# An encoder layer on one core: tokens turned by VectorE instead of TensorE in the projection, with three smaller edits merged in

## The chip, the cores and the metric

The kernel runs on one core of a Trainium2 chip. The metric is the device time of one execution in microseconds (us). A core has five engines that work side by side, each in its own written order: TensorE (PE, matrix products and 128x128 transposes), VectorE (DVE), ScalarE (ACT), GpSimd (POOL) and SyncE (SP, which only issues DMAs here). They wait for each other through semaphores.

## The reference, cut to what matters

One encoder layer over 3,072 tokens (2,048 and 1,024) of 1,024 numbers, in float32. The change touches the normalisation ahead of the first product, rope and, in small ways, what comes after.

```python
def rmsnorm(x, g):
    y = x * lax.rsqrt(jnp.mean(x * x, axis=-1, keepdims=True) + EPS)
    return y * g

def encoder(x, mem, ...):
    z = rmsnorm(x, g_mix) @ w_in                     # 1024 -> 2304 columns
    q_a, k_a = rope(z[..., :512]), rope(z[..., 512:1024]); v_a = z[..., 1024:1536]
    o_a = dilated_attention(q_a, k_a, v_a)           # three patterns, 8 heads
    u, v = split(gelu(z[..., 1536:2048]))            # gMLP: layernorm(v), mixed over 128 tokens
    o_b = u * (w_spatial @ layernorm(v) + b_spatial)
    o_c = softmax(z[..., 2048:] @ k_mem.T) @ v_mem   # attention to 256 memory rows, 4 heads
    x = x + concat(rmsnorm(o_a), rmsnorm(o_b), rmsnorm(o_c)) @ w_out
    x = x + expert_choice(rmsnorm(x, g_ffn), ...)    # 16 experts, each takes its top tokens
    return rmsnorm(x, g_final)
```

## The kernel before, in words

The phases follow each other with a barrier between them: memory (keys and values of the memory rows, and `w_in` split into two parts), projection, attention, mix (`w_out`, norms, router), choice of tokens, experts. Every product in full precision is three passes over a high and a low part of both operands (`hi`, `lo`).

**Projection** (`project_phase`, L321) loops over 24 tiles of 128 tokens, two to a pass of the loop. Each engine has its order written out by hand. TensorE's for tile t: z_qc, the turn of tile t-1's k into [column, token] (`turn_k`, L663), `back` (L669), z_uv, the turn of qc (L695), z_q, the scores to memory (L702), **the turn of tile t+1's x** (`turn`, L656, eight 128x128 transposes into the PSUM tile `ps_x`), z_k, the turn of q (L711), the spatial product (L718, waits for `vln`), the turn of the probabilities (L726, waits for `p_sb`), z_v and the product with the memory's values. All z are `product`, L676.

Before x of tile t+1 is turned, ScalarE squares it (L451) with a sum over its columns, VectorE makes the mean (`mean_x`, L553), GpSimd the power -1/2 (`prep`, L425) and ScalarE scales x by it (`scale_x`, L455). In the [token, column] layout one token is one partition, so a sum is one number per partition. After the turn ScalarE copies `ps_x` out as the high part (`hi_x`, L460) and VectorE subtracts for the low part (`lo_x`, L557).

Beside that runs the chain of gelu and layernorm: ScalarE squares uv (`uv_sq`, L494), VectorE makes `inner` (L587, L589), ScalarE takes the exp (L503), VectorE one plus it, its reciprocal (L593), the product `guv`, mean and variance (L598 to L604), and, behind the rotation of q (`rotate`, L567 and L571) and the row maximum of the scores (L610), `vln` (L618, L622). On ScalarE the scaling of x stands ahead of that exp, and `hi_x` behind it. The exponentials of the scores (L511) give `p_sb`.

SyncE stores v, obc, and the turned q and k of a tile, one DMA each with runs of 512 bytes (L397 to L404), and loads x two tiles ahead (L126).

**Memory phase** (`memory_phase`, L130): SyncE loads `w_in` in 24 pieces of 128 rows and 768 columns (L190), ScalarE and VectorE split each into its two parts (L210, L252). **Mix** (L1113): 24 tiles again; its first loads are issued at its own start (L1171, L1200). **Experts** (L1852): 16 experts of 12 units each; SyncE loads the weights in quarters (L1563). The final norm of 24 token tiles is worked into the last two experts: tile t is loaded at the unit `FIN_AT[t]` (L1957) and squared on ScalarE one unit later (L2110). The first of them in the last expert waits for the previous expert's scatter:

```python
if t == 0 or FIN_AT[t - 1] < M <= FIN_AT[t]:
    sp.wait_ge(s["scattered"], 16 * ST * e)
```

Of the kernel before, what the change touches and what calls it, by code (L numbers as in the profile page):

```python
# [114 lines left out]
class Tokens:  # L115


    def __init__(self, keep):
# [4 lines left out]
        self.s = {n: keep.sem(n) for n in "squared_x meaned_x powered_x scaled_x".split()}  # L123

    def load(self, sp, A, t, u):
        sp.dma_start(self.x[:, u, :], A["x"][bass.ds(t * P, P), :]).then_inc(self.x_loaded[u], 16)  # L126
        sp.dma_start(self.cs[:, u, :, :], A["cossin"][bass.ds(t * P, P), :]).then_inc(self.x_loaded[u], 16)


def memory_phase(nc, A, kmT, vm, w_hi, w_lo, tok):  # L130
# [9 lines left out]
    with Phase(nc, "mem") as ph:  # L140
# [4 lines left out]
        junk = ph.sb("junk", [P, D], BF16)  # L145
# [4 lines left out]
        stat = ph.sb("stat", [P, 3])  # L150
# [7 lines left out]
        ssx, msx, rsx = stat[:, 0:1], stat[:, 1:2], stat[:, 2:3]  # L158
# [12 lines left out]
        with nc.Block() as block:  # L171
            @block.sync
            def _(sp):
# [10 lines left out]
                rows(2)  # L184
                for q in range(PIECES):
# [11 lines left out]
            def _(pool):  # L197
# [5 lines left out]
                nc.gpsimd.tensor_tensor(rsx, msx, half[:, 0:1], ALU.pow).then_inc(tok.s["powered_x"], 1)  # L203

            @block.scalar
            def _(act):
                def hi(q):
                    k, cols = piece(q)
                    act.wait_ge(in_loaded[q % RI], 16 * (q // RI + 1))
# [8 lines left out]
                def square(n):  # L218
                    act.wait_ge(m_loaded[n], 16)
                    ge(act, squared, n)  # L220
                    nc.scalar.activation(junk[:], m[:, n % 2, :], ACT.Square, accum_out=ss[:, n:n + 1]).then_inc(squared, 1)
# [11 lines left out]
                act.wait_ge(tok.x_loaded[0], 32)  # L233
                act.wait_ge(squared, NM)
                nc.scalar.activation(junk[:], x[:, 0, :], ACT.Square, accum_out=ssx).then_inc(tok.s["squared_x"], 1)
# [3 lines left out]
                nc.scalar.activation(x[:, 0, :], x[:, 0, :], ACT.Copy, scale=rsx).then_inc(tok.s["scaled_x"], 1)  # L239
# [3 lines left out]
            def _(dve):  # L243
# [32 lines left out]
                dve.wait_ge(tok.s["squared_x"], 1)  # L276
                nc.vector.tensor_scalar(msx, ssx, 1.0 / D, EPS, ALU.mult, ALU.add).then_inc(tok.s["meaned_x"], 1)
# [6 lines left out]
            def _(pe):  # L284
# [27 lines left out]
                for n in range(NM):  # L312
# [3 lines left out]
                    if n:  # L316
                        turn_k(n - 1)
                turn_k(NM - 1)


def project_phase(nc, A, kmT, vm, w_hi, w_lo, tok):  # L321

    with Phase(nc, "prj") as ph:
# [4 lines left out]
        PADS = 2 * len(SEQS) * PAD // P  # L328
        qkv = ph.sb("qkv", [P, 3, D_A])
# [6 lines left out]
        oc = ph.sb("oc", [P, D_C])  # L336
# [9 lines left out]
        half = ph.sb("half", [P, 2])  # L346
# [475 lines left out]
def attention_blocks():  # L822
# [9 lines left out]
    return blocks  # L832


def attend_phase(nc, A, w_out):

# [1574 lines left out]
```

## Time and profile before

| | |
|---|---|
| median of 3 runs | 3372.18 us (3369.89 to 3373.27) |
| the profiled execution | 3375.52 us, of which the span of the trace is 3373.7 |
| granted TensorE clock, mean of the span | 0.973 |
| busy share of the span | PE 95%, DVE 50%, ACT 43%, POOL 21% |
| projection, from its first to its last instruction | about 53 to 811 us |
| attention, mix, choice of tokens, experts | from about 815, 1,271, 1,645 and 1,708 us |

Busy shares are means over phases with different limits. A granted clock of 1.00 is 2.4 GHz, 0.50 is 1.2 GHz.

### The profile page before, as it was taken

The page shows a single profiled execution, that of the slowest core. Times are in us where ns is not written, and L with a number is a line of the kernel's source. Part 1 is how long each engine was busy: PE and PEld are TensorE (multiplying, and loading weights), DVE is VectorE, ACT ScalarE, POOL GpSimd, SP SyncE. Part 2 cuts the span into 40 slices and gives each one's busy share as a digit, 9 for nine tenths or more (in the row PEclk, how much of TensorE's full clock was granted, in tenths as well). Part 3 has the DMA queues.
Part 4 walks back from the last instruction along what each step waited for, and adds up shares of the span by engine and source line. Part 5 has one row for each costly group of instructions (what it writes and reads, how often), then busy time and mean ns, then how long its engine had stood idle before and what let it go on. Part 6 is the DMA issues. An engine that isn't in the chain of part 4 may idle for free. (4 is left out here: it accounts for less than half of the span.)

```text
span 3373.7 us, 57007 instructions
## 1 busy us (share of the span) xinstructions
PE 3209.9 (95%) x21676; PEld 2892.8 (86%) x21676; DVE 1675.1 (50%) x3594; ACT 1450.6 (43%) x3106; POOL 696.6 (21%) x726
## 2 busy tenths in 40 slices
PE   7999999997999996999579999999999999999996
PEld 5888888886777775888479999999999999999996
DVE  5445445543677775555554443444443444443454
ACT  4333333333788883333333333333333333333443
POOL 0111111112312112222122112222112222112422
PEclk9999999998999997999779999999999999999998
DMA  5111111114744444555347666677666677667895
GB/s 208 59 49 55 51 58 50 48 59 127 248 120 116 127 106 148 191 194 187 113 134 157 137 159 164 164 164 159 137 157 164 164 164 161 136 156 164 231 271 192
DMA packets 345874, 476.41 MB, mean 141 GB/s; under 512 B 31296, under 2 KB 258368, under 8 KB 345536
## 3 DMA queue, kind: packets, MB, share of 16 engines
q1 hardware_dynamic: 324928, 404.34, 43.7%
q0 software_dynamic: 20736, 69.22, 8.3%
q8 instruction: 138, 2.26, 0.3%
q14 instruction: 72, 0.59, 0.1%
HBM read 361.44 MB, written 112.00 MB: 140 GB/s over the span
## 5 line engine op out<-in xcount | busy, mean ns | idle before, releaser
L2127 DVE TENSOR_TENSOR warm_lo<-warm_stage,warm_hi 128x2048 fp32r<-128x2048 f32 x192 | 440.1, 2293 | 596.3 <-ACT warm_hi L1568 596.2
L1568 ACT ACTIVATE warm_hi<-warm_stage 128x2048 fp32r<-128x2048 f32 x192 | 366.5, 1909 | 0.0
L2266 PE MATMUL exp_ps_g<-exp_xT_hi,warm_lo 128*128 128x384 f32 x1024 | 343.1, 335 | 9.7 <-DVE warm_lo L2127 8.2
L2266 PE MATMUL exp_ps_g<-exp_xT_lo,warm_hi 128*128 128x384 f32 x1024 | 342.7, 335 | 0.0
L2266 PE MATMUL exp_ps_g<-exp_xT_hi,warm_hi 128*128 128x384 f32 x1024 | 342.6, 335 | 0.0
L2266 PE MATMUL exp_ps_u<-exp_xT_hi,warm_lo 128*128 128x384 f32 x1024 | 342.0, 334 | 0.0
L2266 PE MATMUL exp_ps_u<-exp_xT_hi,warm_hi 128*128 128x384 f32 x1024 | 342.0, 334 | 0.0
L2266 PE MATMUL exp_ps_u<-exp_xT_lo,warm_hi 128*128 128x384 f32 x1024 | 342.0, 334 | 0.0
L2001 POOL DMA_INDIRECT scratch_y<-exp_ye,route_slots x45 | 92.3, 2052 | 1009.6 <-issue 924.1
L1040 ACT ACTIVATE att_prob<-att_prob,att_o 128x256 f32<-128x256 f32 (+1 forms) x576 | 265.8, 465 | 71.8 <-DVE att_o L1084 68.6
L1976 POOL DMA_INDIRECT exp_xe<-scratch_xn,exp_rows_of x180 | 225.0, 1250 | 55.1 <-issue 54.5
L2083 ACT ACTIVATE exp_hT_hi<-exp_hid 128x768 fp32r<-128x768 f32 x64 | 54.2, 846 | 416.9 <-DVE exp_hid L2160 416.9
L2283 PE MATMUL exp_ps_d<-warm_hi,exp_hT_hi 128*128 128x256 f32 x768 | 217.3, 283 | 0.0
L2283 PE MATMUL exp_ps_d<-warm_hi,exp_hT_lo 128*128 128x256 f32 x768 | 217.3, 283 | 0.0
L2283 PE MATMUL exp_ps_d<-warm_lo,exp_hT_hi 128*128 128x256 f32 x768 | 217.2, 283 | 0.0
L1084 DVE CUSTOM_DVE_ANT_0 att_prob<-att_ps_s,att_masks 128x256 f32<-128x256 f32 (+1 forms) x576 | 183.6, 375 | 40.2 <-issue 40.1
L2266 PEld LDWEIGHTS exp_ps_g<-exp_xT_hi,warm_lo 128*128 128x128 f32 x1024 | 192.8, 188 | 10.2 <-DVE warm_lo L2127 8.5
L2266 PEld LDWEIGHTS exp_ps_g<-exp_xT_lo,warm_hi 128*128 128x128 f32 x1024 | 192.9, 188 | 0.0
L2266 PEld LDWEIGHTS exp_ps_g<-exp_xT_hi,warm_hi 128*128 128x128 f32 x1024 | 192.7, 188 | 0.0
L2266 PEld LDWEIGHTS exp_ps_u<-exp_xT_hi,warm_lo 128*128 128x128 f32 x1024 | 192.2, 188 | 0.0
L2266 PEld LDWEIGHTS exp_ps_u<-exp_xT_lo,warm_hi 128*128 128x128 f32 x1024 | 192.2, 188 | 0.0
L2266 PEld LDWEIGHTS exp_ps_u<-exp_xT_hi,warm_hi 128*128 128x128 f32 x1024 | 192.2, 188 | 0.0
(341 smaller groups left out, 7739.4 us busy)
## 6 DMA issues: line engine op xcount, KB each, us to landing
warm_stage<-in_w_gate SPq DMA_DIRECT2D x256, 256.0 KB, 5.1
warm_stage<-in_w_up SPq DMA_DIRECT2D x256, 256.0 KB, 5.3
warm_stage<-in_w_down SPq DMA_DIRECT2D x256, 256.0 KB, 3.9
mix_o<-scratch_o SPq DMA_DIRECT2D x72, 264.0 KB, 3.0
att_v<-scratch_v SPq DMA_DIRECT2D x64, 256.0 KB, 3.9
scratch_xn<-mix_xn SPq DMA_DIRECT2D x24, 544.0 KB, 3.0
memory_x<-in_x SPq DMA_DIRECT2D x24, 512.0 KB, 3.3
att_v<-scratch_v SPq DMA_DIRECT2D x192, 64.0 KB, 2.2
```

Of the source, the lines that this page charges most:

```text
L1040: x_ = nc.scalar.activation(p, p, ACT.Exp, bias=o[:, c % RO, h:h + 1], scale=-1.0, accum_out=o[:, c % RO, HA + h:HA + h + 1])
L1084: x_ = nc.vector.tensor_tensor_reduce(out=prob[:, n % RP, jj, f, 0:b.W], in0=ps_s[:, n % 2, f, jj, 0:b.W], in1=masks[:, b.mask, 0:b.W], sc ...
L1568: self.nc.scalar.activation(self.hi[:, m % self.RW, :, :], self.stage[:, m % self.RS, :, :], ACT.Copy).then_inc(self.hi_sb, 1)
L1976: nc.gpsimd.indirect_dma_start(xe[:, e % 2, j, a * Q_COLS:(a + 1) * Q_COLS], None, quarters, bass.IndirectOffsetOnAxis(ap=rows_of[:, a, at ...
L2001: nc.gpsimd.indirect_dma_start(A["y"], bass.IndirectOffsetOnAxis(ap=slots[:, j, e:e + 1], axis=0), ye[:, j, :], None, compute_op=ALU.add). ...
L2083: nc.scalar.activation(hT_hi[:, 2 * j:2 * j + 2, :], hid[:], ACT.Copy).then_inc(s["h_hi_sb"], 1)
L2127: nc.vector.tensor_tensor(w_lo[:, m % RW, :, :], stage[:, m % RS, :, :], w_hi[:, m % RW, :, :].bitcast(F32), ALU.subtract).then_inc(s["w_l ...
L2266: x_ = nc.tensor.matmul(ps[:, f, 0:S], a[:, m % RW, k, f * P:(f + 1) * P], b[:, k, :], start=(n == 0), stop=(n == 3 * KC - 1))
L2283: x_ = nc.tensor.matmul(down_banks[j][q][:, 0:UC], b[:, k, rows], a[:, m % RW, k, :], start=(k == 0 and n == 0), stop=(k == KC - 1 and n = ...
```

## The change: what it does, and the diff

The projection loads x of a tile in four DMAs, one for each quarter of the columns. Quarter b lies on partitions 32b to 32b+31, and a token's four quarters lie on four partitions (a token is a lane r of 32 and a group a). In this layout one transposition of every 32x32 block, which VectorE does in one instruction, gives the [column, token] layout that the products want. The rows of `w_in` are loaded in the matching order, by four DMAs a piece, and `g_mix` is laid out to match. The sum of squares of a token now lies on four partitions; a product on TensorE with the constant `lanes` adds them. So squaring, mean, power and scaling each handle four numbers per partition or four quarters. Mean and scaling keep their place in the order of ScalarE; the mean moves behind `inner` on VectorE, `turn_x` stands behind the variance. q and k are likewise turned in 32x32 blocks by VectorE and put right by their stores, four DMAs each with runs of 128 bytes. The factor of the scores goes into the rotation of q, which uses scalar_tensor_tensor. The buffer of oc becomes a part of obc. TensorE's transposes of x, q and k and ScalarE's copies of turned q and k fall away.

Merged with it: the first loads of the mix are issued inside attention, into space that the queries of the first sequence no longer need (`Early`), and the mix's first weighting goes ahead of its weight split; the first expert turns the first half of the columns of all tokens first (`FIRST`), and its first unit waits for half of them at a time; the final-norm tiles of the last expert are loaded later (`FIN_AT`).

```diff
 class Tokens:
     def load(self, sp, A, t, u):
-        sp.dma_start(self.x[:, u, :], A["x"][bass.ds(t * P, P), :]).then_inc(self.x_loaded[u], 16)
+        for b in range(QUADS):
+            sp.dma_start(self.x[b * QR:(b + 1) * QR, u, :].rearrange("t (a c) -> t a c", c=QD),
+                         A["x"][bass.ds(t * P, P), b * QD:(b + 1) * QD].rearrange("(a t) c -> t a c", t=QR)).then_inc(self.x_loaded[u], 16)
@@ memory_phase, SyncE @@
                 for q in range(PIECES):
-                    sp.dma_start(stage[:, q % RI, :], A["w_in"][k * P:(k + 1) * P, cols]).then_inc(in_loaded[q % RI], 16)
+                    for b in range(QUADS):
+                        rows_b = A["w_in"][b * QD + k * QR:b * QD + (k + 1) * QR, cols]
+                        sp.dma_start(stage[b * QR:(b + 1) * QR, q % RI, :], rows_b).then_inc(in_loaded[q % RI], 16)
                     if q == 2 * PER - 1:
+                        sp.wait_ge(squared, NM)
                         tok.load(sp, A, 0, 0)
@@ project_phase, SyncE @@
+                def store_turned(name, which, t, stored):
+                    for a in range(BLOCKS):
+                        part = A[name][:, :, bass.ds(t * P + a * B32, B32)].rearrange("(c i) j t -> i j c t", i=B32)
+                        sp.dma_start(part, qkv[a * B32:(a + 1) * B32, which, :].rearrange("i (j c t) -> i j c t", c=BLOCKS, t=B32))\
+                            .then_inc(stored, 16)
                         sp.wait_ge(s["rotk_sb"], t + 1)
-                            sp.wait_ge(s["xT"], t + 1)
+                            sp.wait_ge(s["lo_sb"], t + 1)
                             tok.load(sp, A, t + 2, u)
+                        sp.wait_ge(s["q_turned"], t + 1)
+                        store_turned("qT", 0, t, q_stored)
@@ project_phase, GpSimd @@
+                        if not is_first(t):
+                            root_bc(t - 1)
                         if not (last and u):
                             prep(t + 1)
-                        if not is_first(t):
-                            root_bc(t - 1)
@@ project_phase, ScalarE @@
                 def square_x(t, u, n):
-                    nc.scalar.activation(probT[:], x[:, u, :].rearrange("p (k c) -> p k c", c=P), ACT.Square, accum_out=ssx).then_inc(s["squared_x"], 1)
+                    for a, x_a in enumerate(tok.quarters(u)):
+                        x_ = nc.scalar.activation(probT[:, 2 * a:2 * a + 2, :], x_a.rearrange("p (k c) -> p k c", c=P), ACT.Square,
+                                                  accum_out=ssx[:, a:a + 1])
+                    x_.then_inc(s["squared_x"], 1)
                 def scale_x(t, u):
                     act.wait_ge(s["powered_x"], t + 1)
-                    nc.scalar.activation(x[:, u, :], x[:, u, :], ACT.Copy, scale=rsx).then_inc(s["scaled_x"], 1)
+                    for a, x_a in enumerate(tok.quarters(u)):
+                        x_ = nc.scalar.activation(x_a, x_a, ACT.Copy, scale=rsx[:, a:a + 1])
+                    x_.then_inc(s["scaled_x"], 1)
                 def hi_x(t, u):
-                    act.wait_ge(s["xT"], t + 1)
+                    act.wait_ge(s["x_turned"], t + 1)
...
-                        if not is_first(t):
-                            out_k(t - 1)
...
-                        nc.scalar.activation(qkv[:, 0, :], ps_c[:], ACT.Copy, scale=SCALE).then_inc(s["qT_sb"], 1)
@@ project_phase, VectorE: functions @@
+                def turn_x(t, u):
+                    dve.wait_ge(s["scaled_x"], t + 1)
+                    nc.vector.transpose(x[:, u, :], x[:, u, :]).then_inc(s["x_turned"], 1)
                 def mean_x(t):
-                    nc.vector.tensor_scalar(msx, ssx, 1.0 / D, EPS, ALU.mult, ALU.add).then_inc(s["meaned_x"], 1)
+                    nc.vector.tensor_scalar(msx, ps_x[:, 0, 0:QUADS], 1.0 / D, EPS, ALU.mult, ALU.add).then_inc(s["meaned_x"], 1)
+                def turn32(which, t, added, done):
+                    dve.wait_ge(added, t + 1)
+                    nc.vector.transpose(qkv[:, which, :], qkv[:, which, :]).then_inc(done, 1)
...
-                        last_a = nc.vector.tensor_tensor(ah[:, :, j, :], zh[:, :, j, :], cos, ALU.mult)
+                        last_a = nc.vector.scalar_tensor_tensor(out=ah[:, :, j, :], in0=zh[:, :, j, :], scalar=scale, in1=cos, op0=ALU.mult, op1=ALU.mult)
@@ project_phase, VectorE: order of a tile @@
-                        if more:
-                            mean_x(t + 1)
                         if not is_first(t):
                             mean_bc(t - 1)
+                            turn32(1, t - 1, s["rotk_sb"], s["k_turned"])
...
                         nc.vector.tensor_tensor(uv_b[:], uv_b[:], ps_b[:], ALU.mult).then_inc(s["inner"], 1)
+                        if more:
+                            mean_x(t + 1)
...
                         nc.vector.tensor_scalar(vev, mv[:, 1:2], EPS, None, ALU.add).then_inc(s["var_eps"], 1)
+                        if more:
+                            turn_x(t + 1, 1 - u)
                         dve.wait_ge(s["z_q"], t + 1)
...
                         if more:
                             lo_x(t + 1, 1 - u)
-                        ge(dve, k_stored, 16 * t)
+                        ge(dve, k_stored, 16 * BLOCKS * t)
+                        turn32(0, t, s["rotq_sb"], s["q_turned"])
@@ project_phase, TensorE @@
+                def sum_x(t):
+                    pe.wait_ge(s["squared_x"], t + 1)
+                    nc.tensor.matmul(ps_x[:, 0, 0:QUADS], tok.lanes[:], ssx, start=True, stop=True).then_inc(s["summed_x"], 1)
...
-                        if not is_first(t):
-                            turn_k(t - 1)
                         product(ps_b, u, 3 * D_A, 2 * D_B).then_inc(s["z_uv"], 1)
+                        if not (last and u):
+                            sum_x(t + 1)
...
-                        if not (last and u):
-                            turn(t + 1, 1 - u)
                         product(ps_a, u, D_A, D_A).then_inc(s["z_k"], 1)
-                        pe.wait_ge(s["rotq_sb"], t + 1)
-                        for j in range(HA // 2):
-                            x_ = nc.tensor.transpose(ps_c[:, j * P:(j + 1) * P], qkv[:, 0, j * P:(j + 1) * P], ident[:])
-                        x_.then_inc(s["qT_ps"], 1)
                         pe.wait_ge(s["vln_sb"], t + 1)
@@ attend_phase, SyncE (LEFT: blocks of the first sequence, RO: buffers of the outputs) @@
+                    if c == LEFT + RO - 1:
+                        sp.wait_ge(q_set, LEFT - 1)
+                        for t in range(2):
+                            early.load_o(sp, A, t, t)
+                        early.load_x(sp, A, 0, 0)
+                        sp.dma_start(early.g_out, A["g_out"]).then_inc(early.g_loaded, 16)
+                        sp.dma_start(early.ident, A["ident"]).then_inc(early.id_loaded, 16)
@@ mix_phase, ScalarE @@
+                weigh(0)
                 act.wait_ge(g_loaded, 16)
-                hi_w(0)
-                weigh(0)
-                hi_w(1, 2, 3, 4, 5)
+                hi_w(0, 1, 2, 3, 4, 5)
@@ expert_phase @@
-        FIN_AT += [M + m for m in (1, 1, 2, 3, 3, 4, 5, 5, 6)]
+        FIN_AT += [M + m for m in (3, 3, 4, 4, 5, 5, 6, 6, 6)]
+        FIRST = [r for half in range(2) for r in range(half, ROUNDS, 2)]
...
-                            if m == 0:
+                            if m == 0 and e:
                                 pe.wait_ge(s["xT_lo_sb"], ROUNDS * (e + 1))
+                                        if e == 0 and m == 0 and f == 0 and k % 4 == 0:
+                                            pe.wait_ge(s["xT_lo_sb"], ROUNDS // 2 * (k // 4 + 1))
```

## Rows read from the trace of the kernel before

**Rows 1.** Stretches: us; busy of PE, PEld, DVE, ACT, POOL; PEclk, DMA share, GB/s.

```profile
200.00:231.15 31.15, 31.15 (x181) 26.04 (x181) 14.81 (x32) 11.19 (x27) 4.34 (x5) 1.00 0.16 53
```

**Rows 2.** Timeline of PE, one projection tile: start us, us, engine, line, out<-in, shape.

```profile
230.03 1.10 PE L656 MATMUL prj_ps_x<-memory_ident,memory_x 128*128 128x128 f32 x8
230.88 0.48 PE L676 MATMUL prj_ps_a<-memory_w_hi,prj_hT_lo 128*128 128x512 f32 x1
...
236.44 0.60 PE L711 MATMUL prj_ps_c<-memory_ident,prj_qkv 128*128 128x128 f32 x4
236.88 1.00 PE L718 MATMUL prj_ps_o<-prj_vln,prj_wsT 128*128 128x64 f32 x8
237.72 1.04 PE L726 MATMUL prj_ps_x<-memory_ident,prj_prob 128*128 128x128 f32 x8
```

**Rows 3.** Timeline of ACT, the same tile.

```profile
220.81 0.51 ACT L475 ACTIVATE prj_obc<-prj_uv_b,prj_stat 128x256 f32<-128x256 f32 x1 [1.12 <-POOL prj_stat L420]
221.22 0.49 ACT L476 ACTIVATE prj_obc<-prj_oc,prj_stat 128x256 f32<-128x256 f32 x1
...
225.18 0.63 ACT L503 ACTIVATE prj_uv_a<-prj_uv_b 128x512 f32<-128x512 f32 x1
...
235.85 0.21 ACT L511 ACTIVATION_READ_ACCUMULATOR prj_prob<-prj_ps_s,prj_stat 128x1 f32 x1
```

**Rows 4.** Timeline of DVE, the same tile.

```profile
224.46 0.69 DVE L589 TENSOR_TENSOR prj_uv_b<-prj_uv_b,prj_ps_b 128x512 f32<-128x512 f32 x1
...
231.10 0.15 DVE L604 TENSOR_SCALAR prj_stat<-prj_stat 128x1 f32<-128x1 f32 x1
231.28 0.76 DVE L567 TENSOR_TENSOR prj_qkv<-prj_ps_c,memory_cs 128x256 f32<-128x256 f32 x2
...
234.52 0.48 DVE L622 SCALAR_TENSOR_TENSOR prj_vln<-prj_vln,prj_stat,prj_ln_b 128x256 f32<-128x256 f32 x1
```

**Rows 5.** Timeline of POOL, memory phase.

```profile
21.66 1.04 POOL L201 TENSOR_TENSOR mem_rstd<-mem_ms,mem_half 128x4 f32<-128x4 f32 x1 [20.82 <-DVE mem_ms L271]
```

**Rows 6.** Groups by line, DVE: busy us, mean ns of one, idle before.

```profile
L2135 DVE STREAM_TRANSPOSE exp_act_g<-exp_xe 128x512 f32<-128x512 f32 x45 | 31.7, 704 | 0.0
```

**Rows 7.** DMA issues at the mix's start: KB each, median us to landing.

```profile
mix_w_r<-in_w_router SPq DMA_DIRECT2D x1, 64.0 KB, 7.2
```

**Rows 8.** Timeline of SP's DMA issues, memory phase and one weight tile.

```profile
6.99 2.62 SPq L190 DMA_DIRECT2D mem_stage<-in_w_in  x5
...
28.13 16.98 SPq L190 DMA_DIRECT2D mem_stage<-in_w_in  x12
...
1718.91 1.91 SPq L1563 DMA_DIRECT2D warm_stage<-in_w_gate  x4
```

**Rows 9.** Timelines of SP and DVE, start of the mix.

```profile
1270.71 1.32 SPq L1171 DMA_DIRECT2D mix_o<-scratch_o  x3
...
1276.61 0.18 DVE L1354 TENSOR_REDUCE mix_stat<-mix_o 128x8 f32<-128x24 f32 x1 [10.34 <-DMA mix_obc<-scratch_obc]
```

**Rows 10.** Timeline of PE, first product of the first expert.

```profile
1725.57 0.41 PE L2266 MATMUL exp_ps_g<-exp_xT_hi,warm_lo 128*128 128x384 f32 x1 [1.56 <-DVE exp_xT_lo L2146]
```

**Rows 11.** Timelines of SP, ACT and PE, last expert.

```profile
3268.15 0.82 SPq L1957 DMA_DIRECT2D exp_fin<-scratch_y  x2
...
3291.65 1.06 ACT L2110 ACTIVATE exp_fin_junk<-exp_fin 128x1024 bf16<-128x1024 f32 x1 [10.72 <-DMA exp_fin<-scratch_y]
...
3300.58 0.69 PE L2266 MATMUL exp_ps_g<-exp_xT_hi,warm_lo 128*128 128x384 f32 x1 [8.15 <-DVE warm_lo L2127]
```

**Rows 12.** PE in the mix, and slices (as rows 1) around two gaps.

```profile
1306.36 0.90 PE L1461 MATMUL mix_ps_c<-mix_ident,mix_oa 128*128 128x128 f32 x3 [5.64 <-ACT mix_oa L1277]
...
1303.00:1304.00 1.00, 0.00 (x0) 0.00 (x0) 0.00 (x0) 0.00 (x0) 0.98 (x1) 0.86 0.00 0
...
3297.00:3298.00 1.00, 0.00 (x0) 0.00 (x0) 0.00 (x0) 1.00 (x1) 0.57 (x1) 0.55 1.08 388
...
3303.00:3304.00 1.00, 1.00 (x5) 1.00 (x5) 1.00 (x2) 0.00 (x0) 1.00 (x2) 0.53 1.03 385
```

More of the change, by code:

```diff
@@ L157, in memory_phase @@
         psK = ph.psum("psK", [P, 4, P])
-        ssx, msx, rsx = stat[:, 0:1], stat[:, 1:2], stat[:, 2:3]
+        ssx, msx, rsx = (stat[:, n * QUADS:(n + 1) * QUADS] for n in range(3))
+        lanes_loaded = ph.sem("lanes_loaded")
         m_loaded = [ph.sem(f"m_loaded{n}") for n in range(NM)]
@@ L317, in _ @@
                         turn_k(n - 1)
+                    if n == NM - 2:
+                        pe.wait_ge(lanes_loaded, 16)
+                        pe.wait_ge(turned_sb, NM - 1)
+                        pe.wait_ge(tok.s["squared_x"], 1)
+                        nc.tensor.matmul(psT[:, 0, 0, 0:QUADS], tok.lanes[:], ssx, start=True, stop=True).then_inc(tok.s["summed_x"], 1)
                 turn_k(NM - 1)
@@ L335, in project_phase @@
         ob = uv_b[:, 0:D_B]
[L336 removed]
+        oc = obc[:, D_B:]
         qc = ph.sb("qc", [P, D_C])
@@ L847, in attend_phase @@
     NU = 2 * NB
+    LEFT = sum(b.seq == 0 for b in blocks)
     with Phase(nc, "att") as ph:
@@ L1169, in load_o @@
                     ge(sp, s["cT_ps"], t - 1)
-                    for j in range(3):
-                        sp.dma_start(o3[:, u, j, :], A[f"o{j}"][bass.ds(t * P, P), :]).then_inc(o_loaded[u], 16)
-                    sp.dma_start(obc[:, u, :], A["obc"][bass.ds(t * P, P), :]).then_inc(o_loaded[u], 16)
+                    early.load_o(sp, A, t, u)
                 def load_x(t, u, n):
@@ L2210, in _ @@
                                         table.pick[:, at:at + 1], ALU.mult, ALU.add).then_inc(s["rows_set"], 1)
-                for r in range(ROUNDS):
-                    lo_x(r, first_banks[r % len(first_banks)])
+                for n, r in enumerate(FIRST):
+                    lo_x(n, r, first_banks[n % len(first_banks)])
                 for m in range(1, RW - 1):
@@ L2286, in _ @@
                 spread_rows()
-                for r in range(ROUNDS):
-                    turn(r)
+                for n, r in enumerate(FIRST):
+                    turn(n, r)
                 pe.wait_ge(s["rows_set"], 1)
@@ L2317, in build @@
             if upto >= 2:
-                attend_phase(nc, A, w_out)
+                early = Early(nc, out)
+                attend_phase(nc, A, w_out, early)
             if upto >= 3:
-                mix_phase(nc, A, affinity, w_out)
+                mix_phase(nc, A, affinity, w_out, early)
         with Phase(nc, "warm") as warm:
```

185 lines of the change are left out of this document (99 added, 86 removed).

## The prediction

> **What bounds the kernel now.** I read the table of stretches first, for one steady token tile of the projection. It shows TensorE busy for the whole 31.15 us period at a granted clock of 1.00, VectorE and ScalarE at less than half of it [rows 1]. So an instruction taken off TensorE there is worth its pitch, and a wait put on it costs its length. The timeline of TensorE in the next tile [rows 2] gives the pitches and the place of the first two waits: the spatial product (L718) waits for `vln`, the transposes of the probabilities (L726) for `p_sb`. The timelines of ScalarE and VectorE [rows 3, 4] show the chain that makes both: gelu's exp (L503), reciprocal, variance (L604), rotation of q (L567), row maximum, `vln` (L622 ends 235.00) and the last exponential's sum (ends 236.06). TensorE gets to the place of L711 at 236.44. With L711 gone, that is where L718 would start. The slack on `vln` is thus 236.44 - 235.00 = 1.44 us.
>
> **Projection: TensorE's own work.** Removed per tile: eight transposes of x (230.03 to 230.88, 0.85 us), four of q (236.44 to 236.88, 0.44) and four of k, which I take at the 0.43 of q's [rows 2]: 1.72 us. Added: one product with `lanes`, four columns wide. The nearest row is L718, where eight records of 64 columns take 236.88 to 237.72, 0.105 us each; two records, as a pair of that row's four groups has, make 0.21. Net -1.51 us a tile, if nothing waits.
>
> **Projection: the chain to `vln`.** Three edits lengthen it. VectorE and ScalarE work in their written order, so nothing of the chain can pass them.
> First, the scaling of x. `mean_x` now stands behind `inner` on VectorE and reads PSUM; `inner` ends at 224.46 + 0.69 = 225.15 [rows 4]. The mean takes the 0.15 of L604, GpSimd's power of 128x4 takes 1.04 [rows 5], and I allow 0.05 for each of three hand-overs (L503 starts 0.03 behind `inner`): 226.49. Then come four scalings of 256 columns on ScalarE, whose pitch is that from L475 to L476, 0.41 [rows 3]: 226.49 + 1.64 = 228.13. Only then does ScalarE reach gelu's exp, which before began at 225.18: 2.95 us later. In the old order mean and power lay ahead of the square of uv, in the wait for z_uv, and the scaling alone stood before the exp.
> Second, `turn_x` stands between the variance and the rotation of q. The nearest row is a 32x32-block transpose of half the width, 0.704 us [rows 6]. Twice that is 1.41, once is the bound below; I take 1.3, as the work grows with columns and a small part doesn't.
> Third, the rotation's four products become scalar_tensor_tensor: 0.48 (L622, as wide) against 0.38 (half of L567's 0.76) [rows 4]; between 0 and 0.4 in all, and 0.2 taken because L622 reads SBUF alone.
> Together 2.95 + 1.3 + 0.2 = 4.45 us (3.65 to 4.76). TensorE meanwhile arrives 0.85 - 0.21 = 0.64 earlier, so 0.80 of slack is left and it stalls 4.45 - 0.80 = 3.65 us (2.85 to 3.96) ahead of L718. Late next is `p_sb`: it comes at 236.06 + 4.45 = 240.51, while L718, released at 239.45, ends 0.84 later at 240.29: another 0.2. A tile costs -1.51 + 3.65 + 0.2 = +2.34 us (1.35 to 2.65). The next chain starts from the next z_uv, so nothing of it is won back. For the 23 tiles that prepare a successor: 53.8; the last saves 0.9 on q and k: **+53 us** (30 to 60).
> Costed at nothing: the quarter squares, the turn of k and the turn of q in 32x32 blocks on VectorE, and `lo_x` from SBUF. The squares and the turn of k lie in the stretch in which ScalarE and VectorE wait for z_uv (L476 ends at 221.71, `inner` starts at 224.46). The turn of q comes behind `vln`, and between L726 and the product that needs VectorE's last copy TensorE has another whole product, z_v (5.56 us, as z_k from 230.88 to 236.44). Without that cover each turn costs 0.7 us a tile. That oc and obc now share a buffer makes VectorE's write of oc wait for the last store of obc, issued a tile before.
>
> **Projection: SyncE.** The eight stores of q and k of a tile now move runs of 128 bytes, 512 to a store. The nearest row for such pieces is a load of 1,024 runs of 64 bytes, landed in 7.2 us with other loads around it [rows 7]: at half of it for each of four, 14.4 us. The stores of k are issued ahead of `inner` (224.46) and asked for behind `vln` (now 239.45), at `turn32(0)`: 15 us. So I cost them at nothing, with little to spare. The load of x goes out later in the tile by the chain's delay; that too I cost at nothing, and a late x would hold ScalarE ahead of `uv_sq` as a late store holds VectorE. The Trainium skill ("DMA: Bandwidth & Descriptors", Specifications) says that transfers under 512 bytes don't reach line rate; by that this edit turns stores that cost nothing into a possible bound, and the time would be that of the rival below. That row is the only one that bears on it, and it leaves room.
>
> **Memory phase.** SyncE issues at 0.52 us a piece (2.62 for five) up to 0.48 (1.91 for a weight tile's four), starts w_in at 6.99 and ends at 45.11 [rows 8]. Before, buffers paced it; now 96 quarter loads, `lanes`, the last memory rows and five loads of x make 103 issues, at 0.478: 49.2, so 56.2 instead of 45.1. **+11 us** (+7 at the 0.44 of the mix's loads [rows 9], +16 at 0.52). Behind the last load stands the split of that piece as before.
>
> **Ends of phases.** k of the last tile goes out in four stores, not one: 3 x 0.48, **+1.4**. The first join of the mix waits for its loads, issued from 1270.71, until 1276.61 [rows 9]; with `Early` they lie in SBUF: **-5.9** (weigh(0) first may add under 1 us; a late landing takes it all). The first expert waits 1.56 us for the last `lo_x` [rows 10], which the new order of rounds can save: **-1.5** (0 to -1.6). In the last expert ScalarE stands until 3291.65 on a final-norm tile, loaded behind SyncE's issue at 3268.15, which waits for a scatter with the weight loads queued behind it, and TensorE starves for 8.15 us up to 3300.58 [rows 11]; after it the clock is low until about 3303.95 [rows 12], 3.4 us at half speed, 1.7 lost. Two slots later the scatter is done when SyncE asks: **-9.8** (0 if the three loads crowded into the last slot block as long).
>
> **Sum.** 53 + 11 + 1.4 - 5.9 - 1.5 - 9.8 = +48 us, on the profiled execution's 3375.5: 3423.7. That execution is 3.3 us above the median of the runs shown, 3372.18, so in their terms **3420 us**; its own range is 3393 to 3442.
>
> **Rivals.**
> (a) *The clock falls in each stall.* At 1306.36 TensorE had been idle for 5.64 us, since 1300.72; the clock fell in the slice 1303 to 1304 (0.86), about 3.0 us into it. In the gap before 3300.58 it fell at about 3297.1 (0.55 in that slice), 4.7 us in [rows 11, 12]. A stall of 3.65 lies between the two. If it falls, 3.4 us of work go at 1.2 GHz, 1.7 us a tile: +39, 3459. The Trainium skill ("TensorE: Matmul & The Clock Gate", HAM oscillation) tells of a wait in every pass of a loop that brings the clock down in every pass: then this is the case. Against it: in the longer gap the clock held for 4.7 us, past the end of such a stall.
> (b) *TensorE stays the bound.* If the chain's three delays stay under the 0.80 of slack, each tile gives its 1.51 us: -36 + 11 + 1.4 - 17.2 = -41, 3331. It takes a ScalarE that gets to gelu's exp before the scaling, or delays a fifth of mine. The whole change breaks even at a stall of 1.7 us, `p_sb` included.
> (c) *Half the stall*, 1 to 2.3 us, by a `turn_x` near 0.7 and a scaling faster than its rows: 3358 to 3390.
> (d) *Small stores bind.* If pieces cost twice the bound of [rows 7], four stores of k need 28.8 us and come 13.8 late at `turn32(0)`. At most all of that reaches TensorE, and less by what z_v covers: some 10 x 23 = +230, 3650. For it speaks the size of the pieces alone; against it that nothing else is then on the queues.
>
> **Chances.** The forecast 0.53; (a) 0.18; (b) 0.14; (c) 0.11; (d) 0.04. About 0.2%, 7 us, is what a measurement of this kernel can tell from none; (c) is split over the three signs: faster 0.18, same 0.05, slower 0.77. The range runs from (c) to (a), 3362 to 3465, and leaves out (b) and (d).
>
> **What would show it.** In the changed profile: gelu's exp some 3 us behind the end of `inner`, not at once; TensorE idle about 3.6 us ahead of the spatial product, released by VectorE's `vln`; a projection tile of 33.5 us; granted clock near 1.00 through tiles (else (a)); SyncE's w_in issues end near 56; the mix's first reduction on VectorE within 1 us of its phase's start, not 5.9; no gap of TensorE in the last expert. The prediction fails if `vln` comes before TensorE asks for it, if the period stands at 29.7, or if SyncE's loads or stores release VectorE.

## The result, and the profile after

| | before | after |
|---|---|---|
| median | 3371.03 us (3368.90 to 3373.27, 4 runs) | 3457.01 us (3450.57 to 3461.04, 4 runs) |
| span of the profiled execution | 3373.7 us | 3459.3 us |
| granted TensorE clock, mean of the span | 0.973 | 0.959 |

The change makes the kernel 2.5% slower: ratio 1.0253, 95% interval [1.0235, 1.0271]. The forecast of 3420 had the direction; the time lies 15 us above the top of its own range, inside the whole one, and close to the 3459 of rival (a).

The waits of TensorE come first: engine, line, out, releaser, us in total, times, the longest. Before, `vln` was not among them.

```profile
PE prj_ps_o L757 <- DVE prj_vln L673: 67.2, 23, 3.0
PE mix_ps_c L1520 <- ACT mix_oa L1337: 21.8, 2, 16.7
...
PE mem_psT L341 <- ACT mem_rows L251: 12.7, 1, 12.7
...
PE exp_ps_g L2294 <- DVE exp_act_g L2266: 7.7, 1, 7.7
...
PE exp_ps_g L2329 <- DVE warm_lo L2188: 4.6, 1, 4.6
```

One steady projection tile as a stretch, with the columns of [rows 1]: 34.42 us in place of 31.15, TensorE idle for 3 us of it, and the clock at 0.95.

```profile
225.70:260.12 34.42, 31.46 (x167) 26.11 (x167) 16.83 (x35) 11.35 (x34) 4.81 (x5) 0.95 0.19 48
```

The chain inside such a tile, from the timelines of VectorE, GpSimd, ScalarE and TensorE (they answer to [rows 2 to 4]).

```profile
221.04 0.69 DVE L636 TENSOR_TENSOR prj_uv_b<-prj_uv_b,prj_ps_b 128x512 f32<-128x512 f32 x1
221.65 0.15 DVE L597 TENSOR_SCALAR prj_stat<-prj_ps_x 128x4 f32<-128x4 f32 x1
...
221.96 1.01 POOL L467 TENSOR_TENSOR prj_stat<-prj_stat,prj_half 128x4 f32<-128x4 f32 x1 [4.19 <-DVE prj_stat L597]
...
223.01 1.71 ACT L501 ACTIVATE memory_x<-memory_x,prj_stat 128x256 f32<-128x256 f32 x4 [2.18 <-POOL prj_stat L467]
224.62 0.62 ACT L544 ACTIVATE prj_uv_a<-prj_uv_b 128x512 f32<-128x512 f32 x1
...
230.59 1.23 DVE L592 STREAM_TRANSPOSE memory_x<-memory_x 128x1024 f32<-128x1024 f32 x1
231.75 0.72 DVE L615 SCALAR_TENSOR_TENSOR prj_qkv<-prj_ps_c,memory_cs 128x256 f32<-128x256 f32 x2
...
233.05 1.21 DVE L661 TENSOR_REDUCE prj_stat<-prj_ps_s 128x4 f32<-128x1024 f32 x1
...
234.92 0.48 DVE L673 SCALAR_TENSOR_TENSOR prj_vln<-prj_vln,prj_stat,prj_ln_b 128x256 f32<-128x256 f32 x1
...
235.46 1.67 PE L757 MATMUL prj_ps_o<-prj_vln,prj_wsT 128*128 128x64 f32 x8 [2.96 <-DVE prj_vln L673]
236.92 1.91 PE L765 MATMUL prj_ps_x<-memory_ident,prj_prob 128*128 128x128 f32 x8
```

`inner` ends at 221.73 and exp starts at 224.62: mean, power and four scalings stand between. (ScalarE squares and scales x in the places where it did before; the mean is VectorE's, and it is the mean that has moved.) `turn_x` puts 1.16 us ahead of the rotation (230.59 to 231.75). `vln` ends at 235.40, and TensorE has waited 2.96 us for it. L757 and L765 then take 1.46 and 1.91 us, where the same eight took 0.84 and 1.04 [rows 2]. The stretches around that wait say why; the last three columns are the granted clock, the DMA share and GB/s.

```profile
230.00:232.50 2.50, 2.50 (x12) 1.72 (x10) 2.42 (x8) 0.64 (x1) 0.55 (x1) 1.00 0.00 0
232.50:235.46 2.96, 0.00 (x1) 0.00 (x1) 2.89 (x7) 1.35 (x6) 1.26 (x1) 1.00 0.00 0
235.46:238.90 3.44, 3.44 (x17) 3.44 (x18) 3.44 (x9) 1.00 (x6) 0.36 (x1) 0.55 0.00 0
238.90:242.00 3.10, 3.10 (x14) 2.49 (x14) 1.01 (x4) 0.99 (x3) 0.92 (x1) 0.95 0.21 65
```

In the wait itself the clock stands at 2.4 GHz (1.00). It falls just after TensorE has begun again, and 3.44 us of work go at 0.55, nearly 1.2 GHz. That costs 0.45 x 3.44 + 0.05 x 3.10 = 1.70 us. A tile: 29.64 without waits (measured in experiment 5) + 2.96 + 1.70 + 0.12 not assigned = 34.42. Twenty tiles take 34.2 to 34.6 us. Three take 36: in them the clock stays low for 6.8 us, not 3.4. Over the 23 tiles the fall comes between 0.1 us before TensorE begins again and 1.7 us behind it.

The memory phase, by the timelines of SyncE and TensorE: the loads of `w_in`, at 0.46 to 0.47 us each (first and third row; the second holds waits for buffers), and the first projection product.

```profile
7.39 9.28 SPq L203 DMA_DIRECT2D mem_stage<-in_w_in  x20
...
20.14 16.01 SPq L203 DMA_DIRECT2D mem_stage<-in_w_in  x28
...
38.55 22.74 SPq L203 DMA_DIRECT2D mem_stage<-in_w_in  x48
...
72.13 0.58 PE L720 MATMUL prj_ps_a<-memory_w_hi,prj_hT_lo 128*128 128x256 f32 x1 [5.02 <-DVE prj_hT_lo L601]
```

The same product in the kernel before:

```profile
57.25 0.58 PE L676 MATMUL prj_ps_a<-memory_w_hi,prj_hT_lo 128*128 128x256 f32 x1 [2.37 <-DVE prj_hT_lo L557]
```

The last load of `w_in` is issued by 61.29, where 56.2 was predicted. Two stretches of the phase, with the columns as above:

```profile
20.00:30.00 10.00, 10.00 (x31) 4.94 (x30) 4.36 (x6) 4.47 (x6) 0.71 (x1) 1.00 1.05 218
...
40.00:50.00 10.00, 2.60 (x8) 1.03 (x6) 5.80 (x7) 3.92 (x5) 0.00 (x0) 0.73 0.73 207
```

The starts of the mix and of the first expert, and the last expert, which answer to [rows 9 to 11].

```profile
1368.96 0.18 DVE L1413 TENSOR_REDUCE mix_stat<-out_qT 128x8 f32<-128x24 f32 x1 [4.50 <-PEq L102]
...
1380.41 1.09 PE L1520 MATMUL mix_ps_c<-out_qT,mix_oa 128*128 128x128 f32 x4 [16.68 <-ACT mix_oa L1337]
...
1813.71 0.41 PE L2329 MATMUL exp_ps_g<-exp_xT_hi,warm_lo 128*128 128x384 f32 x1
...
3377.51 1.06 ACT L2178 ACTIVATE exp_fin_junk<-exp_xe 128x1024 bf16<-128x1024 f32 x1 [11.65 <-DMA exp_xe<-scratch_y,route_slots]
...
3385.20 0.69 PE L2329 MATMUL exp_ps_g<-exp_xT_hi,warm_lo 128*128 128x384 f32 x1 [4.63 <-DVE warm_lo L2188]
```

The mix's first reduction no longer waits for a DMA, the first expert starts without its 1.56 us, and in the last expert ScalarE stands as long as before, now for the gather of the fix tile (rows of the previous expert's tokens, which GpSimd gathers again for their final norm). TensorE's wait for the joined rows at the mix's start, now 16.7 us, was 23.3 before:

```profile
PE mix_ps_c L1461 <- ACT mix_oa L1277: 29.0, 2, 23.3
```

By marks on TensorE's timeline the 85.6 us of span are: first projection product +14.9, projection to `back` +79.1, gap to attention +1.2, attention +2.9, gap to the mix -6.65 (23.33 to 16.68), from there to the first expert -3.4, experts -2.6.

### The profile page after: what moved, and what is told of

The parts are those of the page before. It is cut to its first block and busy times, and to the rows that moved or that the text cites. A ratio compares the mean times of both kernels' runs of the same rounds, so it can differ in the third digit from the quotient of the medians.

```text
span 3459.3 us, 57179 instructions
## 1 busy us (share of the span) xinstructions
PE 3226.3 (93%) x21340; PEld 2896.6 (84%) x21340; DVE 1723.7 (50%) x3666; ACT 1454.5 (42%) x3274; POOL 703.7 (20%) x726
## 2 busy tenths in 40 slices
DMA packets 433571, 476.50 MB, mean 138 GB/s; under 512 B 134224, under 2 KB 349136, under 8 KB 433232
## 5 line engine op out<-in xcount | busy, mean ns | idle before, releaser
L2188 DVE TENSOR_TENSOR warm_lo<-warm_stage,warm_hi 128x2048 fp32r<-128x2048 f32 x192 | 440.1, 2293 | 599.6 <-ACT warm_hi L1627 599.6
```

Of the source, the lines that this page charges most:

```text
L2188: nc.vector.tensor_tensor(w_lo[:, m % RW, :, :], stage[:, m % RS, :, :], w_hi[:, m % RW, :, :].bitcast(F32), ALU.subtract).then_inc(s["w_l ...
```

## Experiments

Each ratio is to the kernel before on the same chip, with its 95% interval.

**1. The wait filled (e1).** Twelve passes of `w_hi` go into a free PSUM tile (PSUM is the memory that TensorE writes) between z_k and the wait for `vln`; their result is used nowhere.

```diff
                         product(ps_a, u, D_A, D_A).then_inc(s["z_k"], 1)
+                        if not (last and u):
+                            pe.wait_ge(s["guv"], t + 1)
+                            for n in range(12):
+                                nc.tensor.matmul(ps_b[:, 0:512], hT_hi[:, u, n % KC, :], w_hi[:, n % KC, 0:512], start=True, stop=True)
```

> The changed kernel with twelve useless passes of 512 columns (into the buffer of z_uv, once gelu is done with it) between z_k and the wait for vln; they take about 2.75 us of the 2.92 us in which TensorE stands there. What is computed stays the same. Theory A (each stall brings the clock down, and the slow stretch behind it costs 1.65 us a tile and 1.5 more in three tiles): a tile of 32.7 us, not 34.4, no slice at 1.2 GHz in the projection, about 42 us less than the changed kernel, 3415. Rival B (the slow stretch has another cause, such as the stores in small pieces or the share of short products): the tile stays at 34.4, 3457. Rival C (useless passes only push later work): the tile grows, 3460 or more.

Measured: 3416.27 us (3413.83 to 3418.38), 1.0117 [1.0100, 1.0134]. The wait that is left:

```profile
PE prj_ps_o L761 <- DVE prj_vln L673: 5.3, 23, 0.4
```

One tile, as a stretch:

```profile
227.07:259.96 32.89, 32.70 (x178) 26.86 (x178) 16.81 (x35) 11.36 (x37) 4.84 (x5) 1.00 0.19 50
```

TensorE comes to the spatial product as late as before (twelve passes of 0.227 us and 0.23 of wait on average make 2.95), and only the clock differs: 1.00, and 1.53 us less a tile. So of the 79 us some 40 are the clock's, and idleness brings it down.

**2 to 4. The chain shortened (e2, e3, e4).** e2 puts the mean ahead of `inner0`, so that the power runs beside VectorE's `inner`. e3 puts `turn_x` behind `vln`, `hi_x` behind the exponentials and `lo_x` to the end of the tile. e4 does both.

```diff
@@ e2, VectorE @@
+                        if more:
+                            mean_x(t + 1)
                         dve.wait_ge(s["uv_sq"], t + 1)
...
                         nc.vector.tensor_tensor(uv_b[:], uv_b[:], ps_b[:], ALU.mult).then_inc(s["inner"], 1)
-                        if more:
-                            mean_x(t + 1)
@@ e3, VectorE @@
                         nc.vector.tensor_scalar(vev, mv[:, 1:2], EPS, None, ALU.add).then_inc(s["var_eps"], 1)
-                        if more:
-                            turn_x(t + 1, 1 - u)
...
                         if more:
-                            lo_x(t + 1, 1 - u)
+                            turn_x(t + 1, 1 - u)
                         dve.wait_ge(s["z_k"], t + 1)
```

> The mean of the next tile's squares moved ahead of the first step of gelu's inner term on VectorE, so that power and scaling start 1.6 us earlier. Theory A: gelu's exp comes 1.6 us earlier, the stall ahead of the spatial product falls from 2.9 to about 1.3 us, which is too short for the clock to fall; a tile of about 31.2 us, 79 us less: 3378. Rival B (slow stretch not from the stall): a tile of 32.8, 37 us less: 3420. Rival D (the chain is not what TensorE waits for): no change, 3457.

> The turn of x on VectorE moved behind vln, the copy of its high part behind the exponentials of the scores, its low part to the end of the tile. Theory A: vln comes 1.2 us earlier, stall 1.7 us; if that holds the clock, a tile of 31.6 us, 69 us less: 3388. If the clock still falls, 33.2 us and 3430, which is also what rival B (slow stretch not from the stall) expects. Rival D: 3457.

> Both moves together. Theory A: 1.6 and 1.2 us off the chain leave a stall of about 0.2 us; TensorE sets the period, a tile of about 30.0 us against 31.15 before the change: about 106 us less than the changed kernel, 3351, faster than the kernel before the change. Rival B: 63 us less, 3394. Rival E (with the chain short, the stores or loads of x set the period): above 31 us a tile, with TensorE released through SyncE.

| version | wait for `vln` in a tile | tiles with a fallen clock | tile without / with the fall | us | ratio |
|---|---|---|---|---|---|
| after | 2.9 to 3.0 | 23 of 23 | - / 34.4 (three 36.0) | 3457.01 | 1.0253 [1.0235, 1.0271] |
| e3 | 1.8 to 2.0 | 14 of 23 | 31.9 / 33.5 | 3418.12 | 1.0126 [1.0110, 1.0143] |
| e2 | 1.3 to 1.5 | 8 of 23 | 31.4 / 33.0 | 3394.16 | 1.0049 [1.0033, 1.0066] |
| e4 | 0.26 to 0.50 | none | 30.4 / - | 3358.35 | 0.9942 [0.9926, 0.9959] |

The waits for `vln` in e2, e3 and e4, in that order:

```profile
PE prj_ps_o L757 <- DVE prj_vln L673: 32.4, 23, 1.5
...
PE prj_ps_o L757 <- DVE prj_vln L671: 43.9, 23, 2.0
...
PE prj_ps_o L757 <- DVE prj_vln L671: 9.2, 23, 0.5
```

The waits add up: e2 takes 1.5 us off, e3 1.0, both 2.5, so the two moves account for the wait but for a remnant. e2 and e3 came 16 and 30 us above what was expected of them, since I held waits of 1.4 and 1.9 us too short for the clock. They are not. The counts are those of the profiled execution; that of e3 took 3407.91 us, 10 less than its median, so the number of falls need not be the same in each. Two tiles of e2, each from the start of L757, the first behind a wait of 1.50 us and the second behind one of 1.33; a third, which starts at 413.37 behind a wait of 1.50, keeps its clock like the second:

```profile
284.60:286.00 1.40, 1.37 (x11) 1.28 (x12) 1.40 (x2) 1.04 (x6) 0.00 (x0) 1.00 0.00 0
286.00:288.10 2.10, 2.10 (x11) 1.91 (x9) 2.10 (x8) 0.00 (x0) 0.39 (x1) 0.53 0.00 0
...
317.50:319.00 1.50, 1.46 (x12) 1.37 (x13) 1.50 (x2) 1.05 (x6) 0.00 (x0) 1.00 0.00 0
319.00:321.00 2.00, 2.00 (x14) 1.74 (x13) 2.00 (x8) 0.00 (x0) 0.37 (x1) 1.00 0.00 0
```

**5. The sum halfway (e11).** On e4, with the fix tile of experiment 7: TensorE issues `sum_x` in the middle of z_uv, and ScalarE scales x ahead of the squares of uv.

```diff
                     for k in range(KC):
+                        if k == KC // 2 and halfway is not None:
+                            sum_x(halfway)
@@ ScalarE @@
+                        if more:
+                            scale_x(t + 1, 1 - u)
                         act.wait_ge(s["z_uv"], t + 1)
...
-                        if more:
-                            scale_x(t + 1, 1 - u)
```

> The version with the mean ahead of inner0 and the turn of x behind vln (3358 us), with the fix tile two slots later, and with the product over lanes halfway through z_uv and the scaling of x ahead of uv's squares on ScalarE. Theory A: the scaling then ends near the end of z_uv, exp comes within 0.5 us of inner, the 0.26 to 0.50 us that are left of the wait go, no tile shows a fallen clock, and a tile takes 29.7 to 30.1 us: 10 to 15 us less than 3358 with the 2 to 6 of the fix tile, 3343 to 3348. If the product in the middle of z_uv waits for ScalarE's squares of x, the gain turns into a wait at that product and 3358 stays.

Measured: 3340.62 us (3337.99 to 3342.73), 0.9896 [0.9880, 0.9913]. A tile:

```profile
240.00:269.64 29.64, 29.64 (x168) 24.61 (x168) 16.79 (x35) 11.25 (x35) 4.84 (x5) 1.00 0.22 55
```

No wait for `vln` is left, and every tile but the last takes 29.63 or 29.64 us: 31.15 - 1.51. So the transposes were worth what the prediction took off for them.

**6. The merge alone (e8).** The kernel before, with the edits to attention, mix and experts, and nothing of the projection.

> The kernel before with the merge alone: the mix's early loads in attention's last part, weigh(0) first, the first expert's rounds by halves, and the final-norm tiles two slots later. Projection and memory phase are those of before. By the marks of the two traces the merge gave -6.65 at the mix's start, -3.4 from there to the first expert, -2.5 in the experts, and attention's +4.2 may belong to it (the loads share the queues there) or to the projection's stores. If attention's belongs to the merge: -8 on the time before; if not: -12.5.

Measured: 3363.77 us (3361.28 to 3369.83, 6 runs), 0.9965 [0.9952, 0.9978], 12 us less. TensorE's waits show two of its sources:

```profile
PE mix_ps_c L1483 <- ACT mix_oa L1300: 22.1, 2, 16.6
...
PE exp_ps_g L2292 <- DVE warm_lo L2151: 5.4, 1, 5.4
```

The way from the mix's first product to the first expert is 1.2 us shorter than before here, 3.4 in the changed kernel. Attention takes 437.0 us from its first to its last score product, as before (437.1), against 440.1 in the changed kernel. So those 3 us are not the merge's. They are no steady cost of the change either: with the same attention e3 shows 435.3, e6 436.7 and e11 439.3. In the changed kernel's profile the clock stands at 0.94 in the second stretch of 60 us of attention, where the two others have 1.00; what brought it down there stays open.

**7. The fix tile later (e6).** `FIX_AT = M + 5` in place of `M + 3`.

> The changed kernel, but the fix tile's squares stand two slots of the last expert later (FIX_AT = M + 5). Theory A, the final-norm tiles no longer hold ScalarE, and the 4.6 us that TensorE still starves in the last expert are the wait for the gather of the fix tile: with it later that gap goes, and the half speed behind it, 4.6 + 1.7: 3457 - 6 = 3451 us, and no gap of TensorE over 1 us in the last expert. Rival, the gather and the tiles share the queue behind the scatter and another tile takes the place: the gap moves and 3457 stays.

Measured: 3454.58 us (3449.87 to 3461.29), 1.0242 [1.0222, 1.0263]. The mechanism shows: L2178 starts at 3380.7 with no wait ahead of it, and the wait on `warm_lo` is gone from TensorE's list. The time does not tell: the expected 6 us lie within the spread of its runs, and the interval overlaps that of the change. In the seven profiles with the fix tile at `M + 3` (the changed kernel, e1 to e5, e10) TensorE's wait on `warm_lo` goes from 1.9 us (e3) to 9.2 (e4). With `M + 5` it is gone in all five profiles; but e7, e11 and e13 have a wait of 2.9 to 3.5 us on `exp_hT_lo` in the last expert instead (0.6 in e12, none in e6), so the expectation's rival is not out.

**8. One DMA for a piece (e5).** The four quarters' rows come in one access pattern (the nested steps by which a DMA walks through memory).

```diff
-                    for b in range(QUADS):
-                        rows_b = A["w_in"][b * QD + k * QR:b * QD + (k + 1) * QR, cols]
-                        sp.dma_start(stage[b * QR:(b + 1) * QR, q % RI, :], rows_b).then_inc(in_loaded[q % RI], 16)
+                    rows_q = A["w_in"].rearrange("(b k t) c -> k b t c", b=QUADS, t=QR)[k, :, :, cols]
+                    sp.dma_start(stage[:, q % RI, :], rows_q).then_inc(in_loaded[q % RI], 16)
```

> The changed kernel, but each piece of w_in comes by one DMA that fetches the four quarters' rows (the same bytes to the same places), 24 issues in place of 96. Theory A, the first projection product is 14.9 us later because SyncE has to issue four loads a piece at 0.46 to 0.47 us: the 72 issues saved are worth 33 us of SyncE, the pieces are again paced by their buffers, and the first projection product stands near 57 us as before the change; the whole takes 3457 - 15 = 3442 us. Theory B, the loads of x in five parts, or the sum over lanes that GpSimd's power and the last splits now wait for, made it late: then the first product comes within 3 us of 72 and the time stays near 3457.

Measured: 3507.68 us (3504.89 to 3509.94), 1.0391 [1.0373, 1.0408]: 50 us slower, which neither theory foresaw. A stretch with nothing else on the queue:

```profile
40.00:47.00 7.00, 4.72 (x7) 2.07 (x8) 3.17 (x3) 2.39 (x4) 0.00 (x0) 0.52 0.26 103
```

The first product, on TensorE's timeline:

```profile
122.02 0.58 PE L719 MATMUL prj_ps_a<-memory_w_hi,prj_hT_lo 128*128 128x256 f32 x1 [5.02 <-DVE prj_hT_lo L600]
```

At 103 GB/s a piece of 384 KB takes 3.82 us, with a quarter (0.26) of the sixteen DMA engines' time in use; loads to 128 partitions moved 398 GB/s in the kernel before (7 to 20 us). The Trainium skill ("DMA: Bandwidth & Descriptors", Why a DMA increments its semaphore by 16 and not by 1) says that a DMA is spread over the largest number of engines, up to 16, that divides the slowest dimension of both its access patterns; the source's is four here, and the share of 0.26 agrees. So this run says nothing on the rate of issue. e7, e4 with this edit and the fix tile, came to 3408.04 us (3403.36 to 3412.05), 1.0093 [1.0077, 1.0110], 50 above e4 for the same reason.

> The version with the mean ahead of inner0 and the turn of x behind vln (3358 us), and with it one DMA a piece of w_in and the fix tile two slots later. If the three sizes add: 3358 - 15 - 6 = 3337 us, projection tiles of 30.3 to 30.5 us as in that version, first product near 57. If the load of x, which goes out early in the memory phase, now collides with the pieces: some 5 us less of the gain, 3342.

**9. Fewer, wider quarter loads (e10).** `RI, CUTS = 3, 2` (buffers, pieces of a row) in place of `5, 3`: 64 loads of 144 KB.

> The changed kernel with w_in cut into two pieces of 1152 columns a row block instead of three of 768, in a ring of three: again one DMA for each quarter, so 64 issues of 144 KB in place of 96 of 96 KB. Theory A, SyncE's rate of issue (0.46 to 0.47 us each) sets the end of the memory phase: 32 issues fewer are 15 us of SyncE, the ring may take some of it back, and the first projection product comes 10 to 15 us earlier, 57 to 62; time 3442 to 3447 us. Rival, the quarter loads run no faster than the 210 GB/s that they show because they reach only 32 partitions each: then the first product stays near 72 and the time near 3457.

Measured: 3457.89 us (3456.18 to 3463.70), 1.0252 [1.0235, 1.0269]; first product at 68.69 us. A stretch of the memory phase:

```profile
40.00:50.00 10.00, 0.66 (x2) 0.29 (x2) 4.86 (x5) 4.97 (x5) 0.00 (x0) 0.53 0.95 238
```

Its loads among the DMA issues, the last number being the median from issue to landing in us:

```profile
mem_stage<-in_w_in SPq DMA_DIRECT2D x64, 144.0 KB, 4.3
```

The rival holds. SyncE now waits 17.5 us for buffers (7.3 in the changed kernel), the DMA engines are at 0.95, and they move 238 GB/s, not 398. In the changed kernel (0.73, 207 GB/s, 2.7 us from issue to landing of 96 KB) SyncE's rate is the limit from 40 us on, but the ceiling of loads to 32 partitions is only 15% above it; from 20 to 30 us the DMA engines are the limit there too (1.05, 218 GB/s). In the kernel before, with loads to 128 partitions:

```profile
7.00:20.00 13.00, 8.61 (x20) 4.49 (x21) 9.24 (x15) 6.83 (x9) 0.00 (x0) 1.00 1.04 398
```

The Trainium skill ("SBUF — State Buffer", Door 1: The DMA port swizzle) says that 32 partitions reach half of SBUF's ports; 238 against 398 agrees roughly, though no run here tells the ports from another cause. e12, e11 with this edit, gave 3338.97 us (3335.27 to 3342.10), 0.9897 [0.9880, 0.9914], the same as e11.

> The version before it with w_in in pieces of 1152 columns as well. If the sizes add: 10 to 15 us less, 3330 to 3337 us.

**10. The rows set in order (e13).** On e11: `w_in` is laid out ahead of the kernel in the lanes' order, and a piece is one load of 128 rows again.

```diff
-        w_in=a["w_in"][0],
+        w_in=a["w_in"][0].reshape(QUADS, KC, QR, D_IN).transpose(1, 0, 2, 3).reshape(D, D_IN),
```

> The version with the halfway product (3341 us), with the rows of w_in laid out in memory, ahead of the kernel, in the order in which the lanes take them, so that each piece is again one DMA of 128 partitions, as before the change: 24 issues of 384 KB. Theory A, the memory phase is late because 32-partition loads, four to a piece, reach 207 to 240 GB/s by SyncE's rate and by their own, where the old loads reached 400: the first projection product comes at 57 to 59 us, 10 to 12 us earlier than the 67.6 to 72.1 of the versions with quarter loads, and the time is 3329 to 3332 us. Rival, what makes it late is the sum over lanes and the five loads of x: then the first product stays above 65 and the time above 3336.

Measured: 3327.49 us (3326.33 to 3331.84), 0.9858 [0.9841, 0.9874], 13 us less than e11, and 1.4% below the kernel before. Laying out the rows is not in this time. The first 13 us of the loads:

```profile
7.00:20.00 13.00, 8.53 (x19) 4.35 (x19) 9.26 (x15) 6.74 (x9) 0.00 (x0) 1.00 1.04 396
```

The first product:

```profile
59.19 0.58 PE L719 MATMUL prj_ps_a<-memory_w_hi,prj_hT_lo 128*128 128x256 f32 x1 [5.02 <-DVE prj_hT_lo L598]
```

The quarter loads thus cost 8 to 13 us: the first product stands at 59.19, against 67.59 to 72.13 in the executions with 96 of them. At most the remaining 1.9 over 57.25 is left for the sum over lanes and the five loads of x; the phase of the kernel before varies by as much (55.95 in e8).

## Why the prediction was right, and where it was off

**The mechanism** was as forecast: TensorE saves 1.51 us a tile (e11: 29.64), and a chain lengthened at three places makes it wait for `vln`.

**The stall was sized 0.7 too long**, 3.65 us against 2.96. Counted from the start of `inner`'s product with ps_b (L636, L589 before), `vln` ends 14.36 us behind it and ended 10.54 behind it before: 3.82 later, where 4.45 was predicted. TensorE is there after 11.46, before after 11.98: 0.52 earlier, where 0.64 was predicted. Of the chain's terms the exp came 2.86 later (2.95 predicted) and `turn_x` took 1.16 up to the rotation (1.3 predicted), which put 1.05 more between variance and rotation than before. The rotation by scalar_tensor_tensor cost nothing: its four products take 1.30 us (231.75 to 233.05), and took 1.34 before (231.28 [rows 4] to 232.62, below); 0.2 was predicted. The "another 0.2" ahead of L765 shows in e4, where L757 and L765 start 1.05 apart, not 0.84. The row maximum of the kernel before:

```profile
232.62 1.22 DVE L610 TENSOR_REDUCE prj_stat<-prj_ps_s 128x4 f32<-128x1024 f32 x1
```

**The step that failed is the clock's.** Rival (a) got 0.18 with the words "in the longer gap the clock held for 4.7 us, past the end of such a stall". That argued from single gaps to a wait that comes again in each tile. The clock held through the waits, as argued (in two of 23 it fell in their last 0.1 us), and fell behind them. The forecast's sum has no term for that. The 1.7 us a tile of rival (a) was right: 23 x 1.70 = 39, and the three longer falls add 5; e1 measured some 40. The page of the Trainium skill named there ("TensorE: Matmul & The Clock Gate", HAM oscillation) tells of waits of some 3 to 5 us that bring the clock down in every pass; here waits of 2.9 us do so too, in 23 tiles of 23. For 1.3 to 2.0 us the runs show a fall in 8 to 14 tiles of 23. Rival (a) said 3459, and 3457 came, though by terms that offset: the projection lost 13 us less than the 92 of that case (the shorter stall), the memory phase 4 more, the merge gave 5 less, attention took 3. So that it came so near is in part luck.

**Memory phase**, +11 predicted, +14.9 in the profiled execution and 10.3 to 14.9 over the executions with 96 loads. The rate of issue was right (0.46 to 0.47 us). The working left out the waits for buffers, 7.3 us in that execution: the issues end at 61.29, not 56.2. It did not see at all that a load to 32 partitions has a ceiling of its own (e10), which is why fewer issues give nothing.

**Merge**: the mix's start -5.9 predicted, -6.65 measured (e8 repeats it: TensorE's wait for the joined rows fell to 16.6, as after). The first expert's -1.5 came. The last expert's -9.8 failed, with -2.6 for all experts: the term took the wait for the final-norm tile as the only one. Behind it stood the fix tile's gather, due in the same unit `M + 3` and behind the same scatter, so that ScalarE still stood 11.65 us and TensorE 4.63. e6 shows that this was what was left. How much TensorE loses there changes from profile to profile (1.9 to 9.2 us, experiment 7), so even the 3.5 saved here is not a steady gain.

**Rivals (b), (c)**: e11 has the tile of (b), and e4 comes near it; the changed kernel has neither, since `mean_x` and `turn_x` stand in the chain. **Rival (d)** is out. A store in runs of 128 bytes landed in 2.1 us, where 3.6 was taken for one and 14.4 for four:

```profile
scratch_qT<-prj_qkv SPq DMA_DIRECT2D x80, 64.0 KB, 2.1
...
scratch_kT<-prj_qkv SPq DMA_DIRECT2D x80, 64.0 KB, 2.1
```

The rule of the Trainium skill on transfers under 512 bytes ("DMA: Bandwidth & Descriptors", Specifications) weighed nothing here: the kernel now sends 134,224 such packets, and no engine waits for these stores.

**Last stores of k**: +1.4 was predicted. The gap ahead of attention, where they fall, grew by 1.2: SyncE issues the four over 2.63 us, the one before over 0.67.

**Unpredicted**: attention's +2.9, which experiment 6 shows to be this execution's, not the change's.

## What to carry to other kernels

Work taken off the bounding engine pays only as far as the chain beside it has slack. Count what the replacement puts into that chain, and place it where the chain waits anyway: here the same instructions in another order turned +2.5% into -0.6% (e4), and a sum issued half a product earlier, with plain loads, into -1.4% (e13). Of this the merge alone has -0.35% (e8): the work taken off TensorE, the point of the change, is by these ratios worth about 0.2% in e4 and 1.1% in e13 (which also has the fix tile later), and cost 2.9% in the first order. A wait of 1.3 to 3 us on TensorE that comes again in each pass is to be priced with a possible fall of the clock behind it, 1.5 to 1.7 us each here. When one blocked transfer is moved, look for the next one behind the same semaphore.

## What the runs showed of the hardware that was not expected

- The granted clock stayed at 1.00 during waits of 2.9 to 3.0 us and fell, in 21 tiles of 23, after the engine had begun again (in two up to 0.1 us before that; in the first tile of e6 1.0 us before). At waits of 1.3 to 1.5 us it fell in 8 tiles of 23, at 1.8 to 2.0 in 14 of 23, at 0.5 and less in none.
- Loads to 32 partitions moved 238 GB/s with the DMA engines at 0.95 (e10), and 218 at 1.05 in the changed kernel; loads to 128 moved 396 to 398. One whose source has an outer dimension of four moved 103.
- A 32x32-block transposition of 128x1024 took 1.235 us on VectorE (mean of 24), one of 128x512 0.705.
- scalar_tensor_tensor with one operand in PSUM took as long as tensor_tensor (four products of 128x256 in 1.30 us).
